# Two-layer decoder trunk on one core: angle tables through PSUM, other orders at the end of attention, in the ranking and in the third norm, and a last output chunk in parts

## The reference

```python
a    = rmsnorm(h)
cols = a @ W_in[i]            # 2844 columns: FoX, NSA and Diff heads
h    = h + concat[FoX | NSA | Diff] @ W_out[i]
h    = h + PEER(rmsnorm(h))   # top 16 of 128 keys twice, top 16 of their sums, 128^2 experts
h    = h + sigmoid(rmsnorm(h) @ W_g[i]) * (p[i] @ W_p[i])
```

## Time and profile before

| | us |
|---|---|
| median of 3 runs (2085.82 to 2087.4) | 2087.31 |
| the profiled execution, its own time | 2084.7 |
| its span, first to last instruction | 2082.8 |
| TensorE busy in the span | 2034.7 (98%) |
| VectorE / ScalarE / POOL busy | 1385.7 / 1004.2 / 817.4 |
| mean granted TensorE clock | 0.995 |

### The profile page before, as it was taken

One profiled execution on the slowest core, in us unless ns is written; L12 is line 12 of the kernel. 1 busy time (PEld: TensorE's weight loads), 2 busy tenths in 40 slices (PEclk: granted clock), 3 DMA queues, 4 the chain that ended last, 5 costly groups with the idle time before them and its releaser, 6 DMA issues.

```text
span 2082.8 us, 41464 instructions
## 1 busy us (share of the span) xinstructions
PE 2034.7 (98%) x15410; PEld 1791.9 (86%) x15410; DVE 1385.7 (67%) x2851; ACT 1004.2 (48%) x1529; POOL 817.4 (39%) x358
## 2 busy tenths in 40 slices
PE   7999999999999999999999999999999999999998
PEld 7989999888888888888898899988888888888887
DVE  6572898997667666444464738989876676655443
ACT  6564444334444444444566644443344444444444
POOL 5636720004444444434555367100143434344344
PEclk9999999999999999999999999999999999999999
DMA  7414433444454555555453144434454555455553
GB/s 262 149 35 171 162 143 123 162 161 180 179 184 179 184 177 184 186 182 195 168 184 141 33 152 162 142 140 155 160 185 178 184 179 183 178 184 191 181 194 109
DMA packets 49214, 342.66 MB, mean 165 GB/s; under 512 B 5840, under 2 KB 6992, under 8 KB 7888
## 3 DMA queue, kind: packets, MB, share of 16 engines
q1 hardware_dynamic: 48672, 337.94, 45.3%
q10 hardware_dynamic: 432, 3.21, 0.4%
HBM read 340.08 MB, written 1.05 MB: 164 GB/s over the span
## 4 chain that ended last, share of the span: by engine, by line
PE 84%; DVE 10%; ACT 2%; issue 2%; POOL 1%; DMA 0%; SPq 0%; DVEq 0%; ACTq 0%; POOLq 0%
PE psum L839 17%; PE psum L470 17%; PE psum L472 16%; PE psum L471 16%; PE psum L841 8%; PE psum L804 2%; PE psum L813 1%; DVE wl L381 1%; PE psum L707 1%; POOL wl L381 1%; DVE psum L1659 1%; PE psum L573 1%; ACT wh L369 1%; PE psum L774 1%; PE psum L571 1%
## 5 line engine op out<-in xcount | busy, mean ns | idle before, releaser
L381 POOL TENSOR_TENSOR wl<-ring,wh 128x1024 fp32r<-128x1024 f32 x336 | 795.2, 2388 | 1223.1 <-ACT wh L369 1223.1
L369 ACT ACTIVATE wh<-ring 128x1024 fp32r<-128x1024 f32 x628 | 643.6, 1047 | 322.0 <-PE psum L472 316.2
L839 PE MATMUL psum<-xx,wh 128*128 128x512 f32 x1504 | 534.1, 399 | 0.0
L841 PE MATMUL psum<-xx,wl 128*128 128x256 f32 x1504 | 419.0, 279 | 0.0
L470 PE MATMUL psum<-wh,Wh 128*128 128x512 f32 (+1 forms) x1056 | 413.0, 391 | 2.5 <-DVE Wl L1807 1.3
L472 PE MATMUL psum<-wh,Wl 128*128 128x512 f32 (+1 forms) x1056 | 408.6, 387 | 0.0
L471 PE MATMUL psum<-wl,Wh 128*128 128x512 f32 (+1 forms) x1056 | 408.1, 386 | 0.0
L381 DVE TENSOR_TENSOR wl<-ring,wh 128x1024 fp32r<-128x1024 f32 x292 | 344.1, 1221 | 61.1 <-ACT wh L369 61.1
L839 PEld LDWEIGHTS psum<-xx,wh 128*128 128x128 f32 x1504 | 282.7, 188 | 63.2
L841 PEld LDWEIGHTS psum<-xx,wl 128*128 128x128 f32 x1504 | 283.4, 188 | 1.1
L470 PE MATMUL psum<-xx,wh 128*128 128x256 f32 (+1 forms) x816 | 235.8, 289 | 3.5 <-DVE wl L381 2.0
(11 more groups left out here) (255 smaller groups left out, 2755.6 us busy)
## 6 DMA issues: line engine op xcount, KB each, us to landing
ring<-stream SPq DMA_DIRECT2D x318, 1024.0 KB, 4.8
arena<-keys ACTq DMA_DIRECT2D x2, 1024.0 KB, 6.5
smr<-rows SPq DMA_DIRECT2D x1, 1090.0 KB, 14.2
smr<-rows ACTq DMA_DIRECT2D x1, 1090.0 KB, 5.2
h<-x SPq DMA_DIRECT2D x2, 512.0 KB, 6.5
out<-h SPq DMA_DIRECT2D x4, 256.0 KB, 2.2
sm<-cols SPq DMA_DIRECT2D x1, 704.0 KB, 10.3
kst<-consts SPq DMA_DIRECT2D x1, 431.5 KB, 9.0
```

What stands on the lines that cost most here:

```text
L369: nc.scalar.activation(wh[:, buffer_of(L, n), c], ring[:, (L * SLOTS + n) % RING, c], ACT.Copy).then_inc(hi_ok, 1)
L381: eng.tensor_tensor(wl[:, b, c], ring[:, (L * SLOTS + n) % RING, c], wh[:, b, c].bitcast(F32), ALU.subtract).then_inc(done, 1)
L839: pe.matmul(bank(4 + e, 512), w[0][:, e, k, :], xx[:, k, :, :].rearrange("p a t -> p (a t)"), start=(k == 0), stop=False, skip_group_check ...
L841: ins = pe.matmul(bank(4 + e, SEQ), w[1][:, e, k, :], xh[:, k, :], start=False, stop=(k == DC - 1), skip_group_check=True)
```

## The change

Seven edits:
- `angk` moves to PSUM, the last reduced angle goes to a PSUM tile `angr`, and the clamp reads it from there.
- End of attention. TensorE: block 1 is turned as soon as seven of the nine POOL operations are done; both `keep_clock(4, 4)` go; block 3 is turned inside `first_chunk`, after its first pass, and the passes are blocks (1, 2), (0), (3). ScalarE: the evacuation of group 5 comes after unit 26 instead of unit 27, the root comes behind the high parts of blocks 1 and 2 and takes scale and bias itself. VectorE: unit 26's copy comes before the squares of the Diff heads, unit 27's before their sum, the scale step is gone, and the low parts of blocks 1 and 2 come before the rest of the Diff chain.
- `values_out(0, 2)`, which stood ahead of the first Gelu, and `values_out(2, 1)`, behind it, become one `values_out(0, 3)` behind it.
- The index conversions move from before the candidates to behind the rank comparisons.
- In the second half of the 16 blocks, VectorE's low parts come one block sooner; TensorE's order is as it was.
- Third norm: the squares are summed by halves of 512 columns before the parts, VectorE adds the two sums with a reduction, and the root takes scale and bias.
- The last gate chunk of the last layer is done for one token tile, then the other, in two PSUM banks; sigmoid, product, addition and store follow by tile, the store in two parts.

```diff
-        ang, angk = ar(A_ANG, T, NANG), ar(A_ANG + T * NANG, T, NANG)
+        ang, angk, angr = ar(A_ANG, T, NANG), bank(3, T, NANG), bank(3, T, NANG, at=SEQ)
...
+            for t in range(T):
+                sp.wait_ge(part_ok, N_PLEG * LAYERS + t)
+                c = slice((N_PLEG - 1) * CHUNK, D)
+                sp.dma_start(rows_out[:, t, c], h[:, t, c]).then_inc(out_st, 16)
...
+            def final_chunk(banks, L, s):
+                wv = [a[:, 0:DC * CHUNK].rearrange("p (k n) -> p k n", k=DC) for a in parts(L, s)]
+                for t in range(T):
+                    for k in range(DC):
+                        if t == 0 and k % (DC // 2) == 0:
+                            half(L, s, 2 * k // DC)
+                        ins = product(bank(banks[t], CHUNK), [a[:, k, t * P:(t + 1) * P] for a in (xh, xl)],
+                                      [a[:, k, :] for a in wv], k == 0, k == DC - 1)
+                    if t == 0:
+                        ins.then_inc(tail_ps, 1)
+                return ins
...
-                pe.wait_ge(nsa_step, NSA_STEPS * (L + 1))
+                pe.wait_ge(nsa_step, NSA_STEPS * (L + 1) - 2)
                 mix_turn(1)
                 unit_values(UNITS - 1)
+                pe.wait_ge(nsa_step, NSA_STEPS * (L + 1))
                 mix_turn(2)
-                keep_clock(4, 4)
                 pe.wait_ge(fox_ok, L + 1)
                 mix_turn(0)
-                keep_clock(4, 4)
-                pe.wait_ge(mix_ok, L + 1)
-                mix_turn(3)
+                def turn_diff():
+                    pe.wait_ge(mix_ok, L + 1)
+                    mix_turn(3)
...
-                        ins = first_chunk(4, L, S_OUT, 4 * L + 1, order=MIX_ORDER)
+                        ins = first_chunk(4, L, S_OUT, 4 * L + 1, turn_diff, MIX_ORDER, ((0, 1), (2,), (3,)))
...
-                    if u >= 7 and u % 4 == 3:
-                        g = (u - 7) // 4
+                    if u == UNITS - 2 or u >= 7 and u % 4 == 3 and u < UNITS - 1:
+                        g = (u - 6) // 4
...
+                first_parts(L, 1, None, range(2), MIX_ORDER)
+                act.wait_ge(ld_const, 16)
                 act.wait_ge(dms_ok, L + 1)
-                act.activation(dst[:, 1, :, :], dst[:, 0, :, :], ACT.Sqrt).then_inc(drt_ok, 1)
-                first_parts(L, 1, None, range(3), MIX_ORDER)
+                act.activation(dst[:, 1, :, :], dst[:, 0, :, :], ACT.Sqrt, scale=1.0 / HD,
+                               bias=kst[:, K_EPS:K_EPS + 1]).then_inc(drt_ok, 1)
+                first_parts(L, 1, None, (2,), MIX_ORDER)
...
                 scores_out(3)
-                values_out(0, 2)
                 lead(0, range(1))
-                values_out(2, 1)
+                values_out(0, 3)
                 lead(0, range(1, 2))
...
+                for c in range(2):
+                    act.wait_ge(half_ok, 2 * L + c + 1)
+                    for t in range(T):
+                        ins = act.activation(ar(A_XN + (2 * c + t) * 512, 512), h[:, t, c * 512:(c + 1) * 512], ACT.Square,
+                                             accum_out=ss4[:, t, c:c + 1])
+                        if c == 1:
+                            ins.then_inc(ss_ok, 1)
                 first_parts(L, 3, norm_weight(L, 2))
                 high(L, S_PLEG + 1)
-                square_rows(L, 2)
...
+                        act.wait_ge(tail_ps, 1)
+                        act.activation(ar(i * 512, CHUNK), bank(i, CHUNK), ACT.Sigmoid, scale=rstd[:, 2, 0:1]).then_inc(sg_ok, 1)
+                        used(act, L, S_PLEG + i)
...
-                for c in PI_C:
+                for k, c in enumerate(PI_C):
                     settle()
-                    step(dve.scalar_tensor_tensor(out=ang[:, :, :], in0=angk[:, :, :], scalar=-c, in1=ang[:, :, :],
-                                                  op0=ALU.mult, op1=ALU.add))
+                    step(dve.scalar_tensor_tensor(out=angr if k == len(PI_C) - 1 else ang[:, :, :], in0=angk[:, :, :], scalar=-c,
+                                                  in1=ang[:, :, :], op0=ALU.mult, op1=ALU.add))
                 settle()
-                dve.tensor_scalar(ang[:, :, :], ang[:, :, :], 3.1415925, -3.1415925, ALU.min, ALU.max).then_inc(ang_ok, 1)
+                dve.tensor_scalar(ang[:, :, :], angr, 3.1415925, -3.1415925, ALU.min, ALU.max).then_inc(ang_ok, 1)
...
+                turned_out(UNITS - 2)
                 settle()
                 dm = heads(mix[:, :, 768:D])
                 tm = ar(A_TMP, T, 4, HD)
                 step(dve.tensor_tensor(tm, dm, dm, ALU.mult))
-                settle()
-                step(dve.tensor_reduce(dst[:, 0, :, :], tm, AX, ALU.add))
+                turned_out(UNITS - 1)
                 settle()
-                dve.tensor_scalar(dst[:, 0, :, :], dst[:, 0, :, :], 1.0 / HD, EPS, ALU.mult, ALU.add).then_inc(dms_ok, 1)
-                for k in range(2):
-                    turned_out(UNITS - 2 + k)
+                dve.tensor_reduce(dst[:, 0, :, :], tm, AX, ALU.add).then_inc(dms_ok, 1)
...
+                feature_major(4 * L + 1, None, range(2), MIX_ORDER)
                 dve.wait_ge(drt_ok, L + 1)
...
-                feature_major(4 * L + 1, None, range(4), MIX_ORDER)
+                feature_major(4 * L + 1, None, range(2, 4), MIX_ORDER)
...
-                for c in range(2):
-                    step(dve.tensor_copy(i16b[:, c].rearrange("p t r h -> p t h r"),
-                                         i16.rearrange("p t (h c) k -> p t h c k", c=2)[:, :, :, c, :]))
...
                     if c == 0:
                         low_lead(EARLY)
+                for c in range(2):
+                    step(dve.tensor_copy(i16b[:, c].rearrange("p t r h -> p t h r"),
+                                         i16.rearrange("p t (h c) k -> p t h c k", c=2)[:, :, :, c, :]))
...
-                    if n in AFTER:
+                    if n < NB // 2 and n in AFTER:
                         low_lead(AFTER[n])
+                    if n + 1 >= NB // 2 and n + 1 in AFTER:
+                        low_lead(AFTER[n + 1])
                     elif n == NB - 2:
                         low_lead(QP)
```

35 lines of the change are left out of this document (25 added, 10 removed).

## The result

The changed kernel takes 2073.46 us (median of four runs, 2071.42 to 2074.29), the kernel before 2087.36 beside it (four runs, 2085.82 to 2088.66): a ratio of 0.9936, 95% interval 0.9924 to 0.9949. The forecast was 2073.2. The profiled execution took 2073.1 us for a span of 2071.3; that of before had a span of 2082.8.

The account below looks back on a forecast made before the run. TensorE, busy 98%, was taken as the bound, so only its idle, filler, half-clock and end time could be won. Seven terms summed to 14.1 us, from a median of 2087.3 to 2073.2; range 2068 to 2080.5.

Parts of the forecast that it names:

- part 5: One-hot stage, each layer: low parts one block sooner remove the 0.23 us stops behind the 1.6 us ones; 0.9 us in all.
- 1 tables: Angle tables, layer 0: PSUM operands free four steps, the cosine's square is held instead; exponential and TensorE 0.7 us sooner.
- 2 attention, at full clock: End of attention, each layer: reordered chains, no fillers, chunk's end 3.5 us sooner; 7.0 us in all, half-clock time included.
- 3 values out: Values out, each layer: first Gelu no longer behind two copies, third expert's high halves 0.35 us sooner; 0.7 us in all.
- 4 conversions: Index conversions, each layer: moved away from POOL, but rank cast and comparison are held instead; 0.2 a layer, 0.4 us.
- clock: End of attention: a half-clock stretch behind the 1.49 us stop in each layer goes, 1.7 us a layer.
- 6 third norm: Third branch's norm, each layer: sigmoid waits for its chunk alone, 1.8 us sooner, both TensorE stops go; 3.1 us in all.
- 7 tail: Last gate chunk at the kernel's end: halved token tiles save 0.9 us, the smaller store 0.4; 1.3 us.
- rival of 2076.6: End of attention: without fillers the first passes may run at 1.2 GHz, costing 1.7 us a layer; chance 0.18.

Follow-up runs that it names:

- attention_end_alone: Kernel before with only the end of attention changed (copies first, later root, three passes, no fillers): 2076.91 us, ratio 0.9956.
- lambdas_before_cosine: Changed kernel with VectorE's products and sum for the lambdas moved ahead of the cosine's square: 2071.72 us, ratio 0.9928.
- tables_unheld: Changed kernel with lambda products and sum ahead of the angles, and the cosine's square reading one operand from PSUM: 2070.82 us, ratio 0.9920.
- fillers_back: Changed kernel with its two blocks of four filler products put back at the end of attention: 2074.41 us, ratio 0.9938.
- copies_first: Kernel before with one move, VectorE copying the probabilities of units 26 and 27 before squaring and summing the Diff heads: 2089.34 us, ratio 1.0007.
- early_sigmoid_table: Changed kernel with a one-column sigmoid on ScalarE between the third norm's root and the wait for the first gate chunk: 2073.64 us, ratio 0.9939.
- third_norm_undone: Changed kernel with the third branch's norm as before (squares behind the high parts, mean by a form POOL holds): 2074.42 us, ratio 0.9940.
- stops_filled: Changed kernel with filler products before the masked rank products (ten) and two one-hot blocks (seven each), both layers: 2068.45 us, ratio 0.9912.
- before_filled: Kernel before with the same fillers as stops_filled: 2083.41 us, ratio 0.9982.
- all_repairs: Changed kernel with tables_unheld, early_sigmoid_table, stops_filled and the square root's table loaded ahead of the output's first two high parts: 2062.92 us, ratio 0.9886.

## Why the prediction was right, and where it was not

Gains by the traces, each stage against the one before it. Stretches at half clock are taken out at 1.7 us each, but for part 5, which is read between `attention_end_alone` and the changed kernel, where neither has one:

| part | forecast | measured |
|---|---|---|
| 1 tables | 0.7 | 1.0 |
| 2 attention, at full clock | 3.6 | 4.0 |
| 3 values out | 0.7 | 0.7 |
| 4 conversions | 0.4 | 0.3 |
| 5 low parts | 0.9 | 1.5 |
| 6 third norm | 3.1 | 1.2 |
| 7 tail | 1.3 | 1.2 |
| sum at full clock | 10.7 | 9.9 |
| clock | 3.4 | 4 |

The runs give 9.2 to 9.8 us at full clock, by the unit; the clock is what is left of the median's 13.9.

**Parts 1 and 4** came out by the mechanism named: POOL holds whichever operation of VectorE stands beside it with all its operands in SBUF (products, but casts and the clamp too), so removing one hold uncovers the next. `lambdas_before_cosine` and `tables_unheld` show the same from both sides. The Trainium skill, page "SBUF — State Buffer", section "Who interferes with whom", gives the rule, and the trace agrees: two SBUF inputs 2.28 us and 4.13 us for two, one from PSUM 0.26 us.

**Part 2** was right in every milestone to 0.35 us. The forecast 7.0 had 3.4 of clock in it; its 3.6 at full clock was 0.4 short. It counted the filler products at some 2.1 us of start-to-start time in each layer; put back into the new order (`fillers_back`) they cost 0.3, since they stand in waits there. One of the moves alone, the copies, carries nothing (`copies_first`); the part alone carries what it does in the whole (`attention_end_alone`).

**Part 5** was right in kind and too small. Beside the kernel with the old low parts (`attention_end_alone`), the ways between TensorE's waits for the one-hot blocks and to the first pair of experts are 9.97 us for 10.35 and 28.59 for 28.96 in layer 1, and shorter by as much in layer 0: 0.75 us a layer, 1.5 in all, above the part's upper end of 1.2. The term took the stops themselves, 0.23 us; each took some 0.15 us more with it, the refilling that part 6 did count.

**Part 6 is the step that failed.** "Root and reciprocal are done by 2056.7, and the sigmoid waits for its chunk alone: 1.8 us sooner." Of the 1.87 us between the chunk's end (2058.7) and the sigmoid (2060.57) in the earlier trace rows, only 0.58 were the root's lateness; the other 1.28 were the load of the sigmoid's table, which is issued with the sigmoid. The step counted both as won. With the root early, the load stands behind the wait for the chunk, and the first sigmoid gained 0.53 us against the transposes of `h` in both layers (0.58 if one counts from the start of the expert pairs). That is 1.1 to 1.2 in all, below the part's own lower end of 1.5. `early_sigmoid_table` shows that the 1.6 us of stops left are this load, `third_norm_undone` that the part as made is worth 1.1 to 1.2.

**The clock** covered for it, and that was luck, as was part 5's surplus. The forecast counted two stretches of half clock, those of the earlier trace rows; by the unit the kernel before loses 13 us of its mean span to the clock (2085.9 less 2072.7), the changed kernel 9. The rival of 2076.6 looked for new stretches in the attention's end; there were none, with fillers or without. In the changed kernel they sit behind the stop of 2.43 us, which was 1.94 before, in both profiles, behind those of 1.57 us in one, and behind stops of 0.58 and 1.11 us in the other; `stops_filled` takes most of them away.

**Open.** Why the attention's end alone gained 7.7 us of clock, by the unit, when in the whole change the clock gained 4 to 5 isn't settled. A stop of one length is followed by half clock in one execution and not in the next (in the two profiles of the changed kernel at 60.0 and 1087.4 us, or at 335.4 and 1362.8, and at 288 and 1315 in both), and a part that shifts later stops may change that as much as its length. What the runs do show is that filling the long stops raised the mean clock in three kernels (`stops_filled`, `before_filled`, `all_repairs`).

## What to carry to other kernels

When a wait is to be shortened, split the time between its end and the next instruction into all that stands there: a table load behind the wait stays when the wait's releaser comes early. Look in the trace on which side of the wait it lies, for here both are found. A dummy call ahead of the wait moves it, but only into time in which the engine is idle; behind other queued work it does nothing. And price a stop of TensorE with what follows it: stops of 1.57 and 2.43 us that could not be avoided were better spent on products of zeros that fit inside them, and runs of one kernel should be compared by span and granted clock together.

## What the runs showed of the hardware

- Runs of one kernel that spread over 10 us (2081.4 to 2091.4 in span, eleven of the kernel before) differ by granted clock, 0.996 to 0.991. With that taken out the standard deviation falls from 3.0 to 0.8 us, and the spread to 2.5.
- Twenty-four filler products in each layer, 5.1 us of TensorE's time (2.1, 1.5 and 1.5), brought the mean clock from 0.9957 to 0.9988 and the median down by 5 to 6 us.
- A stretch at half clock cost 1.1 to 1.65 us in the one-hot stage, where TensorE also waits for VectorE, and stood behind stops of 0.58 to 2.43 us.
- A table load can run behind the wait of its activation (sigmoid: 2.13 us idle, then 1.28 us of load) or ahead of it (exponential: 1.28 us of load, then 1.88 us idle), in the same queue.
